# The first two products behind the third and the fifth norm advance together, each split block serving both

## The chip, the cores and the metric

The kernel runs on one core of one Trainium2 chip. The metric is the device time of one execution in microseconds, the median of the runs shown. The engines are named as in the profile: PE is TensorE's matmul, DVE is VectorE, ACT is ScalarE, POOL is GpSimd, SP is SyncE, which here only issues transfers.

## What is computed

The reference is a transformer block with two attention branches and a mixture of experts, followed by a second block. The change touches two places of the second block, and the reference has these lines for them (all in fp32, 1024 positions of 1024 channels):

```python
def second_block(x, p, g_mix_pre, g_mix_post, w_in, ...):
    h = rms_norm(x, g_mix_pre[l])            # the "third norm", n3
    z = h @ w_in[l]                          # 512 pool columns first, then the others
    ...
    x = x + rms_norm(merged @ w_o[l], g_mix_post[l])     # n4
    h = rms_norm(x, g_ffn_pre[l])            # the "fifth norm", n5
    up = h @ w_up[l]
    gate_h = causal_dwconv(up[..., :D_FF], ffn_conv_w[l], ffn_conv_b[l])
    hid = jax.nn.gelu(gate_h) * up[..., D_FF:]
    x = x + rms_norm(hid @ w_down[l], g_ffn_post[l])
```

## The kernel before, in words

Activations lie transposed: channels in 8 row blocks of 128 partitions, 1024 positions along the free axis (`KD` is 8, `D` and `T` are 1024, `HALF` is 512). A fp32 operand is split into a high and a low part. The weights of a product are one tile of 1024 x 128, loaded into `wraw` (SP), split by POOL into `whi` (line 377) and `wlo` (line 379), both with two slots r = 0 and 1. The activations are in `Ah` and `Al`. One product gives 128 output channels for all positions: for each of 8 row blocks j and each half, three matmuls (lines 405 to 407), 48 in all, summed in the PSUM tile `acc[r]`.

Semaphores tie this together. `w_lo` counts split weights. `w_used` counts finished products; POOL splits the weights of product n once `w_used` has reached n - 1, that is, when the product before the last one is finished, whose slot it reuses. `acc_free[r]` counts the times that `acc[r]` was emptied. Every engine runs its own instructions strictly in the order of the program.

A norm's factor is not applied before these products but when their result is read. So a product needs only the split rows of its input, while the mean square and its root can come later.

**Behind the third norm.** PE transposes the experts' rows (`turn(m)`, line 1918, eight transposes each) alternately into `acc[1]` and `XX`. DVE adds the residual (`C`, line 1959), ACT makes `Ah` (line 596), DVE makes `Al` (line 599), the latter one block behind the former. The product `pool` 0 takes the row blocks as they come (it waits on `n3_lo`), with `turn(j + 2)` issued ahead of block j by `ahead`. Product 1 runs as a whole behind it. DVE sums the eight squares in its order behind all eight rows of `Al` (lines 1967 and 1969), against ACT's squares (line 1943) in two buffers. PE then waits for the last sum, forms the mean into `Y` (`add_mean`, line 574), and only then goes on to product 2. Between products 0 and 1 POOL also waits for all eight transposes and clears `bdr` (line 1903), and SP's loads of the products after the fourth are queued behind that. ACT empties `acc[0]` and `acc[1]` (`raw_out`, line 1869) behind its squares.

**Behind the fifth norm.** DVE makes each row of the sum (`C`, lines 2276 and 2277) and one block later its `Al` (line 599). ACT makes `Ah` and the square. PE does block j of product `ffn0` 0 and then adds the mean of row j into `Y` (`after`). Product 1 is issued in the next part of the program. Behind the last mean come ACT's root (lines 582 and 583), DVE's `newton_step` (lines 589 to 591) with the factor `R5`, and then DVE empties `acc[0]` with a multiplication by `R5` (line 2354). Product 2 needs that.

Of the kernel before, what the change touches and what calls it, by code (L numbers as in the profile page):

```python
# [27 lines left out]
KD = D // P  # L28
NB = T // P
HALF = 512  # L30
# [77 lines left out]
N0 = {}  # L108
# [14 lines left out]
def program(nc, A, out):  # L123
# [3 lines left out]
    def S(name):  # L127
        if name not in sems:
            sems[name] = nc.alloc_semaphore(name=name + suffix)
        return sems[name]  # L130
# [18 lines left out]
    whi = alloc("whi", [P, 2, KD, P], F32R, offset=o_whi)  # L149
    wlo = alloc("wlo", [P, 2, KD, P], F32R, offset=o_wlo)  # L150
    Ah = alloc("Ah", [P, KD, T], F32R, offset=o_ah)
    Al = alloc("Al", [P, KD, T], F32R, offset=o_al)
# [29 lines left out]
    def vec(name, j=0, n=1):  # L182
        return VEC[:, VCOL[name] + j:VCOL[name] + j + n]
# [103 lines left out]
    acc = [nc.alloc_psum_tensor(f"acc{i}", [P, T], F32) for i in range(2)]  # L287
    XX = nc.alloc_psum_tensor("XX", [P, T], F32)
    X = [XX[:, i * HALF:(i + 1) * HALF] for i in range(2)]
    Y = nc.alloc_psum_tensor("Y", [P, T], F32)  # L290
# [17 lines left out]
    w_lo, w_used = S("w_lo"), S("w_used")  # L308
    acc_free = [S("acc_free0"), S("acc_free1")]
# [38 lines left out]
    def take(r):  # L348
        taken[r] += 1
        return taken[r] - 1 or None  # L350

    def product_run(pe, n0, n, ih, il, k=KD, k0=0):
        with pe.Fori(0, n // 2) as i:
            for r in range(2):
                product(pe, n0 + 2 * i + r, r, ih, il, k, k0, free=i + taken[r])
        taken[0] += n // 2
        taken[1] += n // 2
# [32 lines left out]
    def product(pe, n, r, ih, il, k=KD, k0=0, m=P, free=None, ready=None, after=None, ahead=None):  # L390

        pe.wait_ge(w_lo, n + 1)
        if free is not None:
            pe.wait_ge(acc_free[r], free)
        for j in range(k):
            if ahead is not None:
                ahead(j)
            if ready is not None:  # L400
                pe.wait_ge(ready[0], ready[1] + j + 1)
            for h in range(2):
                o = acc[r][0:m, h * HALF:(h + 1) * HALF]
                cols = slice(h * HALF, (h + 1) * HALF)
                pe.matmul(o, whi[:, r, j, 0:m], ih[:, k0 + j, cols], start=(j == 0), stop=False)  # L405
                pe.matmul(o, whi[:, r, j, 0:m], il[:, k0 + j, cols], start=False, stop=False)  # L406
                last = pe.matmul(o, wlo[:, r, j, 0:m], ih[:, k0 + j, cols], start=False, stop=(j == k - 1))  # L407
            if after is not None and j < k - 1:
                after(j)
        last.then_inc(w_used, 1)  # L410
        if after is not None:
            after(k - 1)

    def ada_load(sp, dst, q, k, landed_sem):

        sp.dma_start(dst, A["ada_w"][0, k * P:(k + 1) * P, q * D:(q + 1) * D]).then_inc(landed_sem, 16)
# [17 lines left out]
    @block.gpsimd  # L434
    def _(pool):
        ch = chain(pool, "pool")
        for t, v in ((one, 1.0), (eps, EPS), (ident, 0.0), (identb, 0.0), (causb, 0.0), (strict, 1.0), (onesb, 1.0),
                     (meanD, 1.0 / D), (meanH, 0.0)):
            ch(pool.memset(t[:], v))
        ch(pool.memset(meanH[0:HD, 0:HD], 1.0 / HD))  # L440
        ch(pool.memset(meanH[HD:P, HD:P], 1.0 / HD))
        for t in (ident, identb):
            ch(pool.affine_select(out=t[:], in_=t[:], compare_op=ALU.not_equal, fill=1.0, base=0,
                                  pattern=[[-1, P]], channel_multiplier=1))

        ch(pool.affine_select(out=causb[:], in_=causb[:], compare_op=ALU.is_ge, fill=NEG, base=0,
                              pattern=[[-1, P]], channel_multiplier=1))

        ch(pool.affine_select(out=strict[:], in_=strict[:], compare_op=ALU.is_gt, fill=0.0, base=0,
                              pattern=[[1, P]], channel_multiplier=-1))  # L450
        pool.sem_inc(S("setup"), 1)
# [119 lines left out]
    def add_mean(pe, squares, first, last, done):  # L571

        for h in range(2):
            ins = pe.matmul(Y[:, h * HALF:(h + 1) * HALF], meanD[:], squares[:, h * HALF:(h + 1) * HALF],  # L574
                            start=first, stop=last)
        ins.then_inc(S(done), 1)
# [152 lines left out]
    def _(pe):  # L729
# [68 lines left out]
        for n in range(Q0 + 12):  # L798
            product(pe, n, n % 2, Ah, Al, free=take(n % 2), ready=(S("n1_lo"), 0) if n == 0 else None,
                    m=HD + 16 if n == 5 else P, after=lambda k, n=n: between(n, k))  # L800
            if n == 5:
                pe.wait_ge(S("k_norm"), 1)
                mean_of(SQ[:, 0, :], XX, "k_norm")
# [293 lines left out]

    units = [(kind, j, b) for kind in ("fox", "dsa") for j in range(4) for b in range(NB)]
    groups = [[(c, min(4, b + 1 - c)) for c in range(0, b + 1, 4)] for _, _, b in units for _ in range(2)]
    g0 = [sum(len(g) for g in groups[:s]) for s in range(2 * len(units) + 1)]  # L1100
    nmax, psum = (lambda s: att[:, 0, s % 4:s % 4 + 1]), (lambda s: att[:, 1, s % 4:s % 4 + 1])
# [223 lines left out]
    @block.tensor  # L1325
    def _(pe):
        for r in range(2):
            product(pe, N0["proj"] + r, r, Ah, Al, 4, 4 * r, free=take(r), ready=(S("o_lo"), 4 * r))
        with pe.Fori(0, 7) as m:
            for r in range(2):  # L1330
                product(pe, 2 * m + N0["proj"] + 2 + r, r, Ah, Al, 4, 4 * r, free=m + taken[r])
        taken[0] += 7
        taken[1] += 7
        product(pe, N0["wout"], 0, Bh, Bl, free=take(0), ready=(S("merged"), 0))
        product(pe, N0["wout"] + 1, 1, Bh, Bl, free=take(1))
        product_run(pe, N0["wout"] + 2, 6, Bh, Bl)
# [523 lines left out]
    block = stage.enter_context(nc.Block())  # L1860


    turn_banks = (acc[1], XX)
    gain3 = lambda m: vec("g_mix_pre_2", m)

    def raw_out(act, g):
# [45 lines left out]
    @block.tensor  # L1912
    def _(pe):
        def turn(m):
            if m >= 2:
                pe.wait_ge(S("x2_done"), m - 1)
            for b in range(NB):
                last = pe.transpose(turn_banks[m % 2][:, b * P:(b + 1) * P], G12[:, 0, b, m * P:(m + 1) * P], ident[:])
            last.then_inc(S("y_turned"), 1)

        def ahead(j):
            if j + 2 < KD:
                turn(j + 2)

        pe.wait_ge(S("y_sum"), NB)
        turn(0)
        turn(1)
        product(pe, N0["pool"], 0, Ah, Al, free=take(0), ready=(S("n3_lo"), 0), ahead=ahead)
        product(pe, N0["pool"] + 1, 1, Ah, Al, free=take(1))
        pe.wait_ge(S("n3_sum"), KD)  # L1930
        add_mean(pe, TT[:, 2, :], True, True, "n3_mean")

# [374 lines left out]
    @block.tensor  # L2307
    def _(pe):
        def after(j):
            pe.wait_ge(S("n5_sq"), j + 1)  # L2310
            add_mean(pe, TT[:, j % 2, :], j == 0, j == KD - 1, "n5_sum")
        product(pe, N0["ffn0"], 0, Ah, Al, free=take(0), ready=(S("n5_lo"), 0), after=after)

# [2 lines left out]
    for c in range(CH):  # L2318
        n0 = N0[f"ffn{c}"]
# [12 lines left out]
        @block.tensor  # L2332
        def _(pe):
            if c == 0:
                product(pe, n0 + 1, 1, Ah, Al, free=take(1))
                product_run(pe, n0 + 2, 14, Ah, Al)
            else:
                product_run(pe, n0, 16, Ah, Al)
            product(pe, n0 + 16, 0, Bh, Bl, free=take(0), ready=(S("hid_lo"), 8 * c))
            product(pe, n0 + 17, 1, Bh, Bl, free=take(1))  # L2340
            product_run(pe, n0 + 18, 6, Bh, Bl)
# [237 lines left out]
```

## Time and profile before

| | us |
|---|---|
| median of 3 runs | 3582.59 (3578.93 to 3582.71) |
| the profiled execution's own time | 3582.84 |
| its span, from the first to the last instruction | 3581.1 |
| PE busy | 3191.9 (89%) |
| DVE busy | 2170.1 (61%) |
| ACT busy | 1322.4 (37%) |
| POOL busy | 1028.4 (29%) |
| mean granted TensorE clock | 0.949 of full |

The busy shares are means over stages. All times of stretches below count from the start of the span. In a timeline row the columns are: start, duration, engine, line, operation, tile written and tiles read, form, count, and in brackets the idle time of the engine just before, with what ended it. Consecutive matmuls overlap, so what a matmul costs is the distance from its start to the start of the next.

### The profile page before, as it was taken

Reading aid. Unit: us, or ns where it says so; the run is one execution under the profiler, and the core shown is the slowest. Engines: PE = TensorE matmul, PEld = TensorE weight load, DVE = VectorE, ACT = ScalarE, POOL = GpSimd, SP = SyncE. Lnnn points to the kernel's source line nnn. Section 1 sums busy time; section 2 is a strip of 40 time slices with the busy share of each in tenths; the row PEclk is TensorE's granted clock in tenths of the full one; section 3 lists DMA queues with packets and bytes.
Section 4 is the critical chain, followed back from the end, with each engine's and each line's share of the span. In section 5 each row is a group of like instructions: output and inputs, shape, how many; then the busy total and the mean of one; then the engine's idle time right before and its main releaser. Section 6 shows DMA issues by size and latency. Waiting matters only on the chain. (4 is left out here: it accounts for less than half of the span.)

```text
span 3581.1 us, 45184 instructions
## 1 busy us (share of the span) xinstructions
PE 3191.9 (89%) x15078; PEld 2527.7 (71%) x15078; DVE 2170.1 (61%) x2771; ACT 1322.4 (37%) x1726; POOL 1028.4 (29%) x529
## 2 busy tenths in 40 slices
PE   5889988888886399999959999699799999999868
PEld 4658866555674388888848788588588888888647
DVE  6588875786524599999865655633555154154362
ACT  3345423666302388888720364101311000001141
POOL 2223322000231211111124333344244444344332
PEclk9999999999998699999979999899899999999989
DMA  6312221230231599999961122132311111111213
GB/s 223 82 42 89 71 59 47 95 110 10 88 129 56 218 385 381 376 379 386 345 237 47 59 88 66 31 115 79 112 56 50 47 47 50 50 47 47 102 57 117
DMA packets 348590, 454.47 MB, mean 127 GB/s; under 512 B 33662, under 2 KB 230204, under 8 KB 348484
## 3 DMA queue, kind: packets, MB, share of 16 engines
q1 hardware_dynamic: 334420, 422.68, 34.2%
q10 hardware_dynamic: 4192, 13.63, 1.3%
q0 software_dynamic: 9872, 16.81, 1.3%
q8 instruction: 59, 0.97, 0.1%
q14 instruction: 47, 0.39, 0.0%
HBM read 401.58 MB, written 62.98 MB: 130 GB/s over the span
## 5 line engine op out<-in xcount | busy, mean ns | idle before, releaser
L405 PE MATMUL acc<-Ah,whi 128*128 128x512 f32 x2336 | 934.0, 400 | 74.5 <-DVE Al L599 18.5
L377 POOL TENSOR_TENSOR whi<-wraw,one 128x1024 fp32r<-128x1024 f32 (+3 forms) x214 | 394.3, 1842 | 1868.1 <-PE acc L407 1533.8
L406 PE MATMUL acc<-Al,whi 128*128 128x512 f32 x2336 | 918.5, 393 | 0.0
L407 PE MATMUL acc<-Ah,wlo 128*128 128x512 f32 x2336 | 918.3, 393 | 0.0
L405 PEld LDWEIGHTS acc<-Ah,whi 128*128 128x128 f32 x2336 | 443.7, 190 | 193.9 <-issue 69.9
L379 POOL TENSOR_TENSOR wlo<-wraw,whi 128x1024 fp32r<-128x1024 f32 (+3 forms) x214 | 532.9, 2490 | 16.8
L406 PEld LDWEIGHTS acc<-Al,whi 128*128 128x128 f32 x2336 | 444.1, 190 | 97.0 <-issue 5.1
L407 PEld LDWEIGHTS acc<-Ah,wlo 128*128 128x128 f32 x2336 | 443.4, 190 | 95.2
L1785 DVE TENSOR_TENSOR mlo<-mraw,mhi 128x1024 fp32r<-128x1024 f32 x256 | 306.3, 1224 | 36.5 <-ACT mhi L1735 25.1
L1735 ACT ACTIVATE mhi<-mraw 128x1024 fp32r<-128x1024 f32 x256 | 266.7, 1062 | 73.1 <-PE acc L1680 45.9
L405 PE MATMUL acc<-Bh,whi 128*128 128x512 f32 x640 | 251.2, 393 | 9.1 <-POOL wlo L379 9.1
L407 PE MATMUL acc<-Bh,wlo 128*128 128x512 f32 x640 | 250.0, 391 | 0.0
L406 PE MATMUL acc<-Bl,whi 128*128 128x512 f32 x584 | 229.2, 393 | 0.0
L2410 ACT ACTIVATE TT<-TT 128x1024 f32<-128x1024 f32 x24 | 25.4, 1060 | 498.6 <-DVEq L2362 498.6
L1678 PE MATMUL acc<-mhi,XTh 128*128 128x512 f32 x512 | 204.3, 399 | 4.7 <-DVE mlo L1785 3.7
L1679 PE MATMUL acc<-mlo,XTh 128*128 128x512 f32 x512 | 201.2, 393 | 0.0
L1680 PE MATMUL acc<-mhi,XTl 128*128 128x512 f32 x512 | 201.1, 393 | 0.0
L1628 POOL DMA_INDIRECT Xs<-h2rows,IDC x33 | 43.6, 1322 | 427.4 <-DVE IDC L1817 409.7
L1791 DVE TENSOR_TENSOR mlo<-mraw,mhi 128x1024 fp32r<-128x1024 f32 x128 | 148.2, 1220 | 0.4
L405 PEld LDWEIGHTS acc<-Bh,whi 128*128 128x128 f32 x640 | 120.8, 189 | 37.0 <-POOL wlo L379 12.0
L407 PEld LDWEIGHTS acc<-Bh,wlo 128*128 128x128 f32 x640 | 120.8, 189 | 25.5
L1741 ACT ACTIVATE mhi<-mraw 128x1024 fp32r<-128x1024 f32 x128 | 132.5, 1066 | 14.8 <-PE acc L1699 13.0
(446 smaller groups left out, 4785.0 us busy)
## 6 DMA issues: line engine op xcount, KB each, us to landing
mraw<-in_exp_w SPq DMA_DIRECT2D x512, 256.0 KB, 6.5
mraw<-in_exp_w SPq DMA_DIRECT2D x128, 512.0 KB, 12.0
wraw<-in_w_in SPq DMA_DIRECT2D x72, 512.0 KB, 3.7
wraw<-in_w_up SPq DMA_DIRECT2D x48, 512.0 KB, 3.7
TT<-in_ada_w SPq DMA_DIRECT2D x32, 512.0 KB, 3.7
TT<-gates SPq DMA_DIRECT2D x32, 512.0 KB, 4.4
wraw<-in_w_down SPq DMA_DIRECT2D x24, 512.0 KB, 3.5
adaraw<-in_ada_w SPq DMA_DIRECT2D x16, 512.0 KB, 8.5
```

Source lines behind the costliest of these rows:

```text
L377: ch(pool.tensor_tensor(whi[:, r, 0:k, 0:m], wraw[:, r, 0:k, 0:m], one[:, 0:1].unsqueeze(2).broadcast_to([P, k, m]), ALU.mult))
L379: pool.tensor_tensor(wlo[:, r, 0:k, 0:m], wraw[:, r, 0:k, 0:m], whi[:, r, 0:k, 0:m].bitcast(F32), ALU.subtract).then_inc(w_lo, 1)
L405: pe.matmul(o, whi[:, r, j, 0:m], ih[:, k0 + j, cols], start=(j == 0), stop=False)
L406: pe.matmul(o, whi[:, r, j, 0:m], il[:, k0 + j, cols], start=False, stop=False)
L407: last = pe.matmul(o, wlo[:, r, j, 0:m], ih[:, k0 + j, cols], start=False, stop=(j == k - 1))
L1678: pe.matmul(o, XTh[:, k, :], mhi[:, k, cols], start=(k == 0), stop=False)
L1679: pe.matmul(o, XTh[:, k, :], mlo[:, k, cols], start=False, stop=False)
L1680: last = pe.matmul(o, XTl[:, k, :], mhi[:, k, cols], start=False, stop=(k == UPS - 1))
L1735: act.activation(mhi[:, q, :], mraw[:, q, :], ACT.Copy).then_inc(S("up_hi"), 1)
L1741: act.activation(mhi[:, UPS + j, :], mraw[:, UPS + j, :], ACT.Copy).then_inc(S("down_hi"), 1)
L1785: dve.tensor_tensor(mlo[:, q, :], mraw[:, q, :], mhi[:, q, :].bitcast(F32), ALU.subtract)\
L1791: dve.tensor_tensor(mlo[:, q, :], mraw[:, q, :], mhi[:, q, :].bitcast(F32), ALU.subtract)\
```

## The change

A new function `product_pair` runs two products through the row blocks together: at each j it waits once for the row block and issues the 6 matmuls of product n into `acc[0]` and the 6 of product n + 1 into `acc[1]`. It waits for the split weights of both and for both accumulators before anything else. It replaces products 0 and 1 behind the third norm and behind the fifth. The transposes behind the third norm now go to `Y` and `XX`, since `acc[1]` is in use from the start. `take` counts as before.

```diff
+    def product_pair(pe, n, ih, il, ready, ahead=None, after=None):
+        for r in range(2):
+            pe.wait_ge(w_lo, n + r + 1)
+            free = take(r)
+            if free is not None:
+                pe.wait_ge(acc_free[r], free)
+        for j in range(KD):
+            if ahead is not None:
+                ahead(j)
+            pe.wait_ge(ready, j + 1)
+            for r in range(2):
+                for h in range(2):
+                    o = acc[r][:, h * HALF:(h + 1) * HALF]
+                    cols = slice(h * HALF, (h + 1) * HALF)
+                    pe.matmul(o, whi[:, r, j, :], ih[:, j, cols], start=(j == 0), stop=False)
+                    pe.matmul(o, whi[:, r, j, :], il[:, j, cols], start=False, stop=False)
+                    last = pe.matmul(o, wlo[:, r, j, :], ih[:, j, cols], start=False, stop=(j == KD - 1))
+                if j == KD - 1:
+                    last.then_inc(w_used, 1)
+            if after is not None:
+                after(j)
...
-    turn_banks = (acc[1], XX)
+    turn_banks = (Y, XX)
...
-        product(pe, N0["pool"], 0, Ah, Al, free=take(0), ready=(S("n3_lo"), 0), ahead=ahead)
-        product(pe, N0["pool"] + 1, 1, Ah, Al, free=take(1))
+        product_pair(pe, N0["pool"], Ah, Al, S("n3_lo"), ahead=ahead)
         pe.wait_ge(S("n3_sum"), KD)
         add_mean(pe, TT[:, 2, :], True, True, "n3_mean")
...
-        product(pe, N0["ffn0"], 0, Ah, Al, free=take(0), ready=(S("n5_lo"), 0), after=after)
+        product_pair(pe, N0["ffn0"], Ah, Al, S("n5_lo"), after=after)
...
             if c == 0:
-                product(pe, n0 + 1, 1, Ah, Al, free=take(1))
                 product_run(pe, n0 + 2, 14, Ah, Al)
```

## Rows read from the trace of the kernel before

**Rows 1.** The page: busy time of each engine, share of the span, instructions.
```profile
PE 3191.9 (89%) x15078; PEld 2527.7 (71%) x15078; DVE 2170.1 (61%) x2771; ACT 1322.4 (37%) x1726; POOL 1028.4 (29%) x529
```

**Rows 2.** Timeline of DVE behind the third norm: two successive products are emptied.
```profile
1927.97 1.23 DVE L2090 TENSOR_TENSOR TT<-acc,RG 128x1024 f32<-128x1024 f32 x1 [2.50 <-PE acc L407]
...
1938.85 1.23 DVE L2090 TENSOR_TENSOR TT<-acc,RG 128x1024 f32<-128x1024 f32 x1 [2.50 <-PE acc L407]
```

**Rows 3.** Timeline of PE behind the third norm.
```profile
1846.67 1.10 PE L1918 MATMUL acc<-ident,G 128*128 128x128 f32 x8 [0.45 <-POOL wlo L379]
...
1851.92 1.82 PE L1918 MATMUL XX<-ident,G 128*128 128x128 f32 x8
...
1858.04 1.03 PE L1918 MATMUL XX<-ident,G 128*128 128x128 f32 x8
...
1860.68 1.03 PE L1918 MATMUL acc<-ident,G 128*128 128x128 f32 x8
...
1863.38 1.03 PE L1918 MATMUL XX<-ident,G 128*128 128x128 f32 x8
...
1882.32 1.98 PE L574 MATMUL Y<-TT,meanD 128*128 128x512 f32 x4 [1.20 <-DVEq L1970]
...
1895.05 0.39 PE L405 MATMUL acc<-Ah,whi 128*128 128x512 f32 x1
```

**Rows 4.** Chain of work that ended last, there: start, us, what.
```profile
1868.37 0.62 DVE TT L1967
...
1870.49 2.89 DVE TT L1969
1873.51 3.21 DVE TT L1969
...
1880.98 1.24 DVE TT L1969
```

**Rows 5.** Timeline of POOL behind the third norm.
```profile
1848.55 3.25 POOL L379 TENSOR_TENSOR wlo<-wraw,whi 128x1024 fp32r<-128x1024 f32 x1
...
1870.39 1.89 POOL L377 TENSOR_TENSOR whi<-wraw,one 128x1024 fp32r<-128x1024 f32 x1 [4.09 <-PE acc L407]
1872.36 3.27 POOL L379 TENSOR_TENSOR wlo<-wraw,whi 128x1024 fp32r<-128x1024 f32 x1
```

**Rows 6.** Stretches: length, busy time of each engine, PEclk granted, DMA share.
```profile
1850.00:1853.50 3.50, 3.50 (x15) 2.92 (x13) 2.73 (x2) 1.15 (x1) 1.79 (x1) 0.51 0.12 33
...
2572.00:2577.20 5.20, 5.20 (x11) 3.08 (x11) 4.98 (x5) 1.69 (x2) 0.00 (x0) 0.51 0.35 142
...
2555.00:2558.90 3.90, 3.78 (x4) 1.17 (x4) 0.00 (x0) 0.07 (x1) 0.00 (x0) 0.50 0.00 0
```

**Rows 7.** Timeline of PE behind the fifth norm.
```profile
2571.93 0.77 PE L405 MATMUL acc<-Ah,whi 128*128 128x512 f32 x1 [13.13 <-DVE Al L599]
...
2577.20 0.80 PE L405 MATMUL acc<-Ah,whi 128*128 128x512 f32 x1
...
2578.99 1.88 PE L574 MATMUL Y<-TT,meanD 128*128 128x512 f32 x4
2580.30 0.79 PE L405 MATMUL acc<-Ah,whi 128*128 128x512 f32 x1
...
2600.12 1.88 PE L574 MATMUL Y<-TT,meanD 128*128 128x512 f32 x4
...
2612.76 0.39 PE L405 MATMUL acc<-Ah,whi 128*128 128x512 f32 x1
```

**Rows 8.** Timeline of DVE behind the fifth norm: two rows of `Al`, newton, `acc[0]` emptied.
```profile
2582.16 1.28 DVE L599 SCALAR_TENSOR_TENSOR Al<-C,VEC,Ah 128x1024 fp32r<-128x1024 f32 x1
...
2586.05 1.28 DVE L599 SCALAR_TENSOR_TENSOR Al<-C,VEC,Ah 128x1024 fp32r<-128x1024 f32 x1
...
2604.32 1.50 DVE L589 SCALAR_TENSOR_TENSOR TT<-TT 128x1024 f32<-128x1024 f32 x1 [7.65 <-ACTq L584]
...
2608.57 1.23 DVE L2354 TENSOR_TENSOR TT<-acc,TT 128x1024 f32<-128x1024 f32 x1 [0.24 <-DVE TT L591]
```

## The prediction

> **What bounds the kernel now.** I read the page first: PE is busy 3191.9 of 3581.1 us [rows 1]. Steady work there is a row of products. Two are emptied 10.88 us apart, and each time DVE had waited for PE [rows 2]. So a product of 48 matmuls costs 10.88, one matmul 0.2267, six 1.36 and twelve 2.72. While PE sets the pace like this, a delay ahead of it is handed on in full to the end. The question is when product 2 can start in each of the two places, and at which clock.
>
> Behind the third norm I read the timelines of PE and POOL and then the chain. The third transposition, at 1846.67, waited for the first split weights. From then on PE and DVE go nearly in step, 2.64 us for a transposition and a block of six matmuls (1858.04 to 1860.68). The last transposition is at 1863.38, the mean at 1882.32, and product 2 is finished at about 1895.05 [rows 3]. The reader should see who released the mean: DVE's queue, after an idle 1.20. The chain runs through the sum of squares, not through product 1, which filled that time [rows 3, 4].
>
> Behind the fifth norm PE first waits 13.13 for a row of `Al`. A block with its mean then costs 3.10 (2577.20 to 2580.30), of which the mean is 1.31. The last mean starts at 2600.12 and product 2 at 2612.76 [rows 7]. In between lies product 1, and beneath it, hidden, the way from the mean to the emptied `acc[0]`: DVE's first newton step at 2604.32, the emptying at 2608.57 until 2609.80 [rows 8], 9.68 after the mean's start.
>
> **The change, part by part.** No matmul, transposition or transfer is added or removed. Product 1 moves from behind the blocks to between them. That fills PE's waits there, and it makes everything that hung on the end of a block six matmuls later, seven or eight times over. It also uncovers what product 1 covered.
>
> *Third norm, the start.* The pair waits for the second split weights too. POOL finishes them at 1848.55 + 3.25 = 1851.80 [rows 5]. The third transposition is queued behind that wait, so it goes from 1846.67 to about 1851.9, and DVE's next residual row waits for it.
>
> *The clock.* From 1850.0 to 1853.5 the granted clock was 0.51, after a partly idle stretch; behind the fifth norm it was 0.51 until 2577.20, 5.2 us after work began again, and in the mean at 2555.0, which had waited for a sum of DVE's, it was 0.50 [rows 6]. These are the 1.2 GHz level against 2.4. I let each idle stretch of 5 us and more be followed by 5.2 us at half speed, worth 2.6; 3.5 us, worth 1.75, is the lower bound.
>
> *Third norm, the blocks.* At half speed the transposition takes about 1.75 (1.82 lasts the one at 1851.92, 1.03 the ones at full clock [rows 3]), to 1853.65. By 1857.1 eight matmuls are done at 0.43, and the other four take 0.9: the next transposition is at 1858.0 instead of 1851.92. From here a period is 2.64 + 1.36 = 4.00, more than DVE's own, so PE sets it. The last transposition comes four periods later, at 1874.0 instead of 1863.38, or 10.6 late. Blocks 5, 6 and 7 end the pair at 1874.0 + 4.00 + 2 x 2.72 = 1883.4. Product 1 ended at about 1881.1 before (1882.32 less the idle 1.20).
>
> *What is late next: the sum.* DVE adds squares only behind all its rows, so its first sum goes from 1868.37 to about 1879.0. That is the core of my forecast: the pair stretches DVE's rows by what it puts between them, and the sum comes behind them. In the old order the sum had one split of POOL's beside it. Two sums took 2.89 and 3.21 instead of 1.24 [rows 4], while POOL's two instructions ran from 1870.39 to 1875.63 [rows 5], a surcharge of 3.6. Now `w_used` rises for both products within 1.4 us, so POOL does two splits in a row from about 1882.1, in the middle of the sums: between nothing more and a second 3.6. I take the whole, since four POOL instructions and five sums meet. The mean is then 10.6 + 3.6 = 14.2 late, at 1896.5. PE has been idle for 13 us, so mean and product 2 start at half speed: 2.6 more. ACT empties `acc[0]` behind its squares and ahead of the mean as now, and product 2's weights are split by 1888; neither ends last. **Sum: +16.8**, with 11.5 if the surcharge doesn't double and both slow stretches are short (-3.6, -0.85, -0.85), and 19 if the third transposition's stretch also holds up the first rows.
>
> The Trainium skill says of this sharing (SBUF — State Buffer, section "Who interferes with whom") that a DVE instruction with two SBUF inputs and a GpSimd instruction that reads SBUF exclude each other for the whole instruction. By that, the surcharge doubles; by a reading of the rows as one chance collision, it stays at 3.6 and the total falls by 3.6.
>
> *POOL's and SP's queues.* POOL's clearing of `bdr` waits for the last transposition and moves with it, from just behind 1863.38 to about 1875 [rows 3], still 5 us ahead of the next split. SP's loads behind it move by the same 10.6. They serve products from the fifth on, which are far off: nothing.
>
> *Banks.* `Y` in place of `acc[1]` for the transposition: same shapes, and the mean writes `Y` long after its last reader. Nothing. If the bank cost something, it would be within DVE's slack of 4.00 against 2.64 a period.
>
> *Fifth norm, the blocks.* Both weights were split long ago. Block 0 starts at 2571.93 and is now twelve matmuls at half speed, to 2577.2. The mean takes 1.31, to 2578.5. A period is 3.10 + 1.36 = 4.46 against the 3.89 of DVE's three instructions (2582.16 to 2586.05 [rows 8]), so PE sets it again. The last mean starts at 2578.5 + 6 x 4.46 + 3.15 = 2608.4, or 8.3 late [rows 7]. PE is done at 2609.7, three microseconds before the old 2612.76: this is the gain that the pair does make.
>
> *What is late next: the root.* The way from the mean to the emptied `acc[0]` is 9.68 [rows 8], with nothing left to cover it: 2608.4 + 9.7 = 2618.1. POOL's two splits, from 2607.0, now lie beside the newton steps, of which two read two SBUF tiles. The first was held for some 0.3 before (1.50 [rows 8]); held behind one POOL instruction each they cost up to 1.3, as each of the sums did. I take 1.3 of the range 0 to 2.5. Product 2 starts at 2619.4 instead of 2612.76, +6.6, and after an idle 9.7 at half speed, +2.6. **Sum: +9.2**, between 7.0 (no collision, short slow stretch) and 11.
>
> The Trainium skill (TensorE: Matmul & The Clock Gate, section "Loop structure matters more than you think") says that DVE copying a result out of PSUM doesn't break PE's warmth. By that the last 2.6 would be absent and the total 2.6 lower. The rows speak against it here, as PE has nothing else to do: behind the 13.13 that it waited for DVE [rows 7] it got 0.51 [rows 6].
>
> **Total.** 16.8 + 9.2 = 26.0 on the profiled execution's own time of 3582.84 (its span of 3581.1 and 1.7 around it), which is 0.25 above the median: 3608.8, as a median 3608.6. The bounds give 3582.6 + 18.5 = 3601 and 3582.6 + 30 = 3613.
>
> **The rivals.**
> *A, the gain arrives.* What follows isn't uncovered: the sum keeps up with the pair and `acc[0]` is emptied in time. Behind the third norm the pair ends at 1883.4, 2.3 late, or with no slow stretch at 1880.8, 0.3 early; behind the fifth it ends 3.0 early. That is -3.3 to -0.7, 3579 to 3582, not slower. It speaks for it that PE does wait on `Al` in both stretches. Against it: DVE's order puts the sums behind the rows, and 9.68 from the mean to the emptied `acc[0]` has nothing above it. It decides only if both hidden chains end before the pair does: from a last sum at 1883 and a root chain of 1.3 on. To be faster by over 0.2% no mechanism in these rows suffices.
> *B, only the third norm loses.* If the clock doesn't fall in the new waits and the splits don't collide with sums or newton steps, what stays is 10.6 and 5.4 (8.3 + 9.7 less 12.6): +16, 3598.6. For it: one surcharge was all that the sums saw. Against it: rows 6.
> *C, the delay grows.* The half-speed stretch spreads, or DVE's rows are held by POOL's late splits as well: each further slow stretch is 2.6 and each held DVE instruction 1.3 to 2. Five of them give +35, 3617.
>
> **How the numbers follow.** The likeliest, +18.5 to +30, gets 0.77; B, down to +10, 0.11; C 0.05; A 0.04, and a mechanism that I don't see, with a gain over 0.2%, 0.03. The measurement can tell about 0.2% (7 us) from no change. So slower has 0.93, same 0.04, faster 0.03. The range is 3599 to 3615: it holds the likeliest, its bounds, and the upper part of B.
>
> **What would show it.** The third transposition at about 1851.9 and the last at 1874; the first sum at 1879 and its last at about 1895; a wait of PE's for DVE's queue of some 13 us ahead of the mean (1.20 before); PEclk near 0.5 for some 5 us behind it. Behind the fifth norm, the last mean at about 2608.4 plus the delay so far, then a wait of PE's of 8 to 10 us that ends with DVE's line that empties `acc[0]` (in the old numbering 2354). Outside the two places nothing but shifts. The prediction is wrong if the mean waits less than 5 us, or if product 2 behind the fifth norm starts right behind the last mean.

## The result, and the profile after

The changed kernel takes 3607.75 us (median of 4 runs, 3605.04 to 3609.15), against 3580.76 for the kernel before on the same chips (4 runs, 3578.78 to 3582.71). The ratio is 1.0073, 95% interval 1.0061 to 1.0085: slower by 26 us, between 22 and 30 (the two medians differ by 27.0). The profiled execution took 3605.04.

The page of the changed kernel: the span, and the busy time of the engines.

```profile
span 3603.3 us, 45184 instructions
...
PE 3194.9 (89%) x15078; PEld 2532.0 (70%) x15078; DVE 2172.5 (60%) x2771; ACT 1322.2 (37%) x1726; POOL 1027.7 (29%) x529
```

The busy time of PE is nearly the same (3191.9 before [rows 1]), in a span that is 22.2 longer. The loss is waiting, and a few us of half speed.

To compare traces I use two stretches between fixed instructions of DVE. *Stretch 3* runs from the first residual row behind the experts to the first emptying of a product of the next run of products. *Stretch 5* runs from the last emptying of the merged branches to the second emptying of an `ffn0` gate product. Their ends in the kernel before, timeline of DVE:

```profile
1844.62 1.28 DVE L1959 SCALAR_TENSOR_TENSOR C<-acc,MOD,RG 128x1024 f32<-128x1024 f32 x1 [2.20 <-PE acc L1918]
...
1917.01 1.23 DVE L2090 TENSOR_TENSOR TT<-acc,RG 128x1024 f32<-128x1024 f32 x1 [26.22 <-PE acc L407]
...
2462.43 1.22 DVE L2240 TENSOR_TENSOR TT<-TT,acc 128x1024 f32<-128x1024 f32 x1 [8.72 <-PE acc L407]
...
2623.84 1.22 DVE L2354 TENSOR_TENSOR TT<-acc,TT 128x1024 f32<-128x1024 f32 x1 [3.78 <-PE acc L407]
```

And in the changed kernel:

```profile
1843.01 1.28 DVE L1981 SCALAR_TENSOR_TENSOR C<-Y,MOD,RG 128x1024 f32<-128x1024 f32 x1 [2.20 <-PE Y L1941]
...
1929.39 1.23 DVE L2112 TENSOR_TENSOR TT<-acc,RG 128x1024 f32<-128x1024 f32 x1 [26.23 <-PE acc L407]
...
2474.58 1.22 DVE L2262 TENSOR_TENSOR TT<-TT,acc 128x1024 f32<-128x1024 f32 x1 [8.73 <-PE acc L407]
...
2645.37 1.22 DVE L2375 TENSOR_TENSOR TT<-acc,TT 128x1024 f32<-128x1024 f32 x1 [4.30 <-PE acc L407]
```

Stretch 3 went from 72.39 to 86.38, +13.99; stretch 5 from 161.41 to 170.79, +9.38. The trace of the changed kernel runs 1.61 early at its start (1843.01 against 1844.62), and one adds that when comparing its times with rows of before.

**Behind the third norm**, timeline of PE in the changed kernel, to be read beside [rows 3]:

```profile
1850.34 1.94 PE L1941 MATMUL Y<-ident,G 128*128 128x128 f32 x8 [5.74 <-POOL wlo L379]
...
1856.34 1.03 PE L1941 MATMUL XX<-ident,G 128*128 128x128 f32 x8
...
1859.98 1.04 PE L1941 MATMUL Y<-ident,G 128*128 128x128 f32 x8
...
1870.86 1.03 PE L1941 MATMUL XX<-ident,G 128*128 128x128 f32 x8
...
1893.13 3.55 PE L597 MATMUL Y<-TT,meanD 128*128 128x512 f32 x4 [12.65 <-DVEq L1992]
```

The third transposition waited 5.74 for POOL's second split. The periods are 3.64 (1856.34 to 1859.98), of which the twelve matmuls take 2.85, from 1857.13 on; before, six took 1.50 (1859.18 to 1860.68). So a matmul in the pair costs no more than one outside it, which leaves rival P of the experiments below (the blocks themselves are dearer) nothing to stand on here. The mean waited 12.65 for DVE's last sum, where it had waited 1.20 before, and its four records take 3.55 instead of 1.98, at half speed. The sums of DVE and the splits of POOL in the same stretch, timelines, to be read beside [rows 4, 5]:

```profile
1876.60 16.43 DVE L1991 TENSOR_TENSOR TT<-TT 128x1024 f32<-128x1024 f32 x7
...
1879.27 1.89 POOL L377 TENSOR_TENSOR whi<-wraw,one 128x1024 fp32r<-128x1024 f32 x1 [5.50 <-PE acc L431]
1881.24 3.21 POOL L379 TENSOR_TENSOR wlo<-wraw,whi 128x1024 fp32r<-128x1024 f32 x1
1884.41 2.87 POOL L377 TENSOR_TENSOR whi<-wraw,one 128x1024 fp32r<-128x1024 f32 x1
1887.36 3.21 POOL L379 TENSOR_TENSOR wlo<-wraw,whi 128x1024 fp32r<-128x1024 f32 x1
```

Two splits now stand back to back beside the sums.

**Behind the fifth norm**, timeline of PE, beside [rows 7]:

```profile
2584.07 0.76 PE L429 MATMUL acc<-Ah,whi 128*128 128x512 f32 x1 [13.13 <-DVE Al L622]
...
2590.60 0.80 PE L429 MATMUL acc<-Ah,whi 128*128 128x512 f32 x1
...
2595.07 0.79 PE L429 MATMUL acc<-Ah,whi 128*128 128x512 f32 x1
...
2620.68 1.88 PE L597 MATMUL Y<-TT,meanD 128*128 128x512 f32 x4
...
2631.64 0.80 PE L405 MATMUL acc<-Ah,whi 128*128 128x512 f32 x1 [9.08 <-DVEq L2376]
```

A period is 4.47 (3.10 before), the last mean comes 36.61 behind the first block (28.19 before), and product 2 then waits 9.08 for the emptied `acc[0]`. The timeline of DVE shows the way there, beside [rows 8]:

```profile
2624.87 1.91 DVE L612 SCALAR_TENSOR_TENSOR TT<-TT 128x1024 f32<-128x1024 f32 x1 [12.32 <-ACTq L607]
...
2630.30 1.22 DVE L2375 TENSOR_TENSOR TT<-acc,TT 128x1024 f32<-128x1024 f32 x1 [0.24 <-DVE TT L614]
```

The stretches from the two restarts on show the clock, beside [rows 6]. The columns are length, the busy times of PE, PEld, DVE, ACT and POOL, then PEclk, the busy share of DMA and its GB/s:

```profile
1893.10:1896.50 3.40, 3.37 (x5) 1.50 (x5) 0.00 (x0) 0.00 (x0) 0.00 (x0) 0.53 0.20 60
2631.60:2637.00 5.40, 5.36 (x13) 4.26 (x14) 4.60 (x4) 1.06 (x1) 0.00 (x0) 0.50 0.13 40
```

PEclk is 0.53 and 0.50, the 1.2 GHz level: for about 3.4 us and 5.4 us both restarts run at half speed.

### The profile page after: what moved, and what is told of

Read it like the earlier page. It is cut to its first block and busy times, and to the rows that moved or that the text cites. A ratio compares the mean times of both kernels' runs of the same rounds, so it can differ in the third digit from the quotient of the medians.

```text
span 3603.3 us, 45184 instructions
## 1 busy us (share of the span) xinstructions
PE 3194.9 (89%) x15078; PEld 2532.0 (70%) x15078; DVE 2172.5 (60%) x2771; ACT 1322.2 (37%) x1726; POOL 1027.7 (29%) x529
## 5 line engine op out<-in xcount | busy, mean ns | idle before, releaser
L405 PE MATMUL acc<-Ah,whi 128*128 128x512 f32 x2272 | 907.4, 399 | 65.0 <-DVEq L2188 14.8
L406 PE MATMUL acc<-Al,whi 128*128 128x512 f32 x2272 | 895.1, 394 | 0.0
L407 PE MATMUL acc<-Ah,wlo 128*128 128x512 f32 x2272 | 894.4, 394 | 0.0
L405 PEld LDWEIGHTS acc<-Ah,whi 128*128 128x128 f32 x2272 | 432.6, 190 | 176.2 <-issue 54.2
L379 POOL TENSOR_TENSOR wlo<-wraw,whi 128x1024 fp32r<-128x1024 f32 (+3 forms) x214 | 533.3, 2492 | 16.8
L406 PEld LDWEIGHTS acc<-Al,whi 128*128 128x128 f32 x2272 | 432.5, 190 | 93.7 <-issue 4.3
L407 PEld LDWEIGHTS acc<-Ah,wlo 128*128 128x128 f32 x2272 | 432.0, 190 | 92.1
```

The source lines that it names most:

```text
L379: pool.tensor_tensor(wlo[:, r, 0:k, 0:m], wraw[:, r, 0:k, 0:m], whi[:, r, 0:k, 0:m].bitcast(F32), ALU.subtract).then_inc(w_lo, 1)
```

## The experiments

The stretches of all traces, in us, with the time of the median run and the ratio to the kernel before on the same chip:

| kernel | stretch 3 | stretch 5 | median | ratio (95%) |
|---|---|---|---|---|
| before | 72.39 | 161.41 | 3580.76 | |
| before, second trace | 72.26 | 161.41 | 3579.11 (one run) | |
| the change | 86.38 | 170.79 | 3607.75 | 1.0073 (1.0061 to 1.0085) |
| the change, second trace | 86.39 | 170.79 | 3608.03 (one run) | |
| third norm alone | 86.85 | 161.45 | 3596.43 | 1.0043 (1.0026 to 1.0060) |
| fifth norm alone | 72.26 | 170.75 | 3590.89 | 1.0031 (1.0019 to 1.0042) |
| mean behind product 2 | 84.03 | 170.47 | 3604.45 | 1.0069 (1.0053 to 1.0086) |
| fourth split later | 82.94 | 170.84 | 3602.50 | 1.0061 (1.0044 to 1.0078) |
| PE kept busy | 86.78 | 169.08 | 3604.37 | 1.0070 (1.0055 to 1.0085) |
| pair's waits later | 83.23 | 170.48 | 3600.44 | 1.0057 (1.0042 to 1.0073) |
| third norm alone, two repairs | 81.30 | 161.41 | 3591.53 | 1.0031 (1.0019 to 1.0042) |
| one block put between | 74.59 | 160.08 | 3585.66 | 1.0015 (1.0006 to 1.0024) |
| mean behind product 2, emptying earlier | 77.18 | 171.12 | 3598.06 | 1.0051 (1.0036 to 1.0066) |
| one block put between, emptying earlier | 71.07 | 160.05 | 3580.13 | 0.9998 (0.9989 to 1.0007) |

A time differs from another of the same kernel by up to 9 us (the kernel before ran from 3575.3 to 3584.7 on one chip); in two traces of one kernel the two stretches repeat within 0.13. Between kernels with the same code in a place they differ more: 86.38 and 86.85 for stretch 3, 170.47 to 171.12 for stretch 5. So a stretch tells 1 us apart, which a median can't.

**Each place alone.** In the first kernel the fifth norm has its two products as before, in the second the third norm.

```diff
-        product_pair(pe, N0["ffn0"], Ah, Al, S("n5_lo"), after=after)
+        product(pe, N0["ffn0"], 0, Ah, Al, free=take(0), ready=(S("n5_lo"), 0), after=after)
...
+                product(pe, n0 + 1, 1, Ah, Al, free=take(1))
```

> The pair behind the third norm alone; the fifth norm's part is as in the kernel before. Theory U (each pair uncovers a chain that product 1 had covered: the sum of squares here, the root there) says the two places are independent: this one costs 14.0 us, as the trace of the change shows between the first transposition and the first emptied product behind it, so about 3595. Rival P (the pair's own blocks are dearer, through the weight slots or the bank Y, wherever they stand) says the same here, since the blocks are the same. Rival D (one place's delay is partly made up, or made worse, by the other) says that this run and the next do not add up to the change.

> The pair behind the fifth norm alone. Theory U: +9.4 us (last mean 8.4 late, acc[0] emptied another 1.2 late, 2.7 for the half-speed stretch behind the idle 9.1, less the 3.1 by which the pair ends early is no gain), so about 3590. Rival D: under 6 or over 13, and the sum with the run before is not that of the change (about 26).

Stretch 3 alone +14.46, stretch 5 alone +9.34, and each leaves the other where it was (161.45 and 72.26). The medians, 1.0043 and 1.0031, add up to 1.0074 against 1.0073. The places are independent within this accuracy, so rival D falls.

**The mean behind product 2.** PE does product 2 before it waits for the sum.

```diff
-        pe.wait_ge(S("n3_sum"), KD)
-        add_mean(pe, TT[:, 2, :], True, True, "n3_mean")
...
-        product_run(pe, N0["pool"] + 2, 10, Ah, Al)
+        product(pe, N0["pool"] + 2, 0, Ah, Al, free=take(0))
+        pe.wait_ge(S("n3_sum"), KD)
+        add_mean(pe, TT[:, 2, :], True, True, "n3_mean")
+        product(pe, N0["pool"] + 3, 1, Ah, Al, free=take(1))
+        product_run(pe, N0["pool"] + 4, 8, Ah, Al)
```

> The change, with PE's wait for the last sum and the mean of the third norm moved from ahead of product 2 to behind product 2. Theory U: PE no longer waits 12.65 us for the sum. Product 2 then waits for POOL's split, which ends about 5.2 us after product 0's last matmul, so some 4 us behind the pair's end. Product 2 starts 8 to 9 us earlier than in the change and without the half-speed stretch of 1.6: 9 to 10 us faster than the change, about 3598. Rival P: the loss is in the pair's blocks, at most 3 us come back, about 3605.

Only 2.35 came back in stretch 3 (86.38 to 84.03), not 9 to 10. My expectation failed, and rival P's figure was the one met. The timelines of PE, ACT and POOL in this kernel say why:

```profile
1889.18 0.76 PE L405 MATMUL acc<-Ah,whi 128*128 128x512 f32 x1 [10.14 <-POOL wlo L379]
...
1887.98 1.01 ACT L1892 ACTIVATE UP<-acc 128x1024 f32<-128x1024 f32 x1
...
1879.80 3.21 POOL L379 TENSOR_TENSOR wlo<-wraw,whi 128x1024 fp32r<-128x1024 f32 x1
...
1885.92 3.21 POOL L379 TENSOR_TENSOR wlo<-wraw,whi 128x1024 fp32r<-128x1024 f32 x1
```

Product 2 waited 10.14, put down to POOL's split. But the split for product 2 was finished at 1883.01 (1879.80 + 3.21). The one for product 3 ended at 1889.13, 0.05 ahead of the start; product 2 doesn't wait for it, as the next run shows. What ended at 1888.99, 0.19 ahead of the start, is ACT's emptying of `acc[0]`. It stands behind ACT's eight squares, and these wait for DVE's sums. So a second way from the sums to product 2 lay close beneath the first: in the change ACT is done with `acc[0]` 2.7 ahead of the mean.

Of the 2.35, some 0.6 lie ahead of the sums, where nothing was edited: these start 32.98 behind the first residual row (1875.20 less 1842.22) against 33.59 in the change (1876.60 less 1843.01).

**That way tested.** The same kernel, with ACT's emptying of `acc[0]` behind its fifth square.

```diff
             act.activation(TT[:, m % 2, :], C[:, m, :], ACT.Square).then_inc(S("n3_sq"), 1)
-        for g in range(2):
-            raw_out(act, g)
+            if m == 4:
+                raw_out(act, 0)
+        raw_out(act, 1)
```

> The change with the mean of the third norm behind product 2, and ACT's emptying of acc[0] placed behind its fifth square instead of behind its eighth. The run with the mean behind product 2 gave 2.4 us in that stretch where theory U had expected 9 to 10, and in its trace product 2 started 0.2 us behind ACT's emptying of acc[0], which stands behind squares that wait for the sums. Theory Q (that queue of ACT's is the second thing that product 1 covered): product 2 now starts when POOL's split is done, 6 us earlier, so the stretch from the first residual row to the first emptied product of the next run falls from 84.0 to 77 or 78 us, and the time to about 3597. Rival P (the pair's blocks, or the clock behind the wait, are the rest): the stretch stays above 82.

Stretch 3 fell by another 6.85 to 77.18, and the median to 3598.06. Timelines of PE, ACT and POOL:

```profile
1884.14 0.50 PE L405 MATMUL acc<-Ah,whi 128*128 128x512 f32 x1 [4.02 <-POOL wlo L379]
...
1879.93 1.00 ACT L1892 ACTIVATE UP<-acc 128x1024 f32<-128x1024 f32 x1
...
1880.88 3.21 POOL L379 TENSOR_TENSOR wlo<-wraw,whi 128x1024 fp32r<-128x1024 f32 x1
```

Now POOL's split for product 2 really ends last, at 1884.09, and product 2 starts while the split for product 3 still runs. The two edits gave back 9.2 of the 14.0 us of stretch 3, 0.6 of them by the scatter between builds. So the larger part of the loss is the ways that lead through the sums, and rival P is out as its cause. What is left, 4.8, holds the late third transposition (tested below), PE's wait of 4.02 for the split, and the lower clock behind this wait (0.63 for 4.6 us).

**The fourth split later.** POOL's split for product 3 waits for the last sum.

```diff
+            if j == 3:
+                pool.wait_ge(S("n3_sum"), KD)
             split(pool, N0["pool"] + j, j % 2, landed[N0["pool"] + j])
```

> The change, with POOL's fourth split (for product 3) made to wait until the third norm's sum is done, so that only one split lies beside the sums. Theory U with the surcharge per split: the seven sums take 13.1 us as before instead of 16.4, the mean comes 3.3 us earlier, and product 3's split still ends under product 2: 3.3 us faster than the change, about 3604. Rival S (the surcharge comes from something else than POOL, such as ACT's squares): the sums stay at 16.4 and the time at 3607.

Timeline of DVE:

```profile
1878.12 13.03 DVE L1993 TENSOR_TENSOR TT<-TT 128x1024 f32<-128x1024 f32 x7
```

The seven sums take 13.03 instead of 16.43, and stretch 3 is 3.44 shorter. So a second split beside the sums costs 3.4, and the surcharge comes from POOL, as expected against rival S. The Trainium skill (SBUF — State Buffer, section "Who interferes with whom") says that a DVE instruction with two SBUF inputs contends with a GpSimd instruction that reads SBUF, and that the ports they share are an exclusive lock. The traces agree: the two held sums of before took 1.65 and 1.97 longer than the free one of 1.24 [rows 4], each about as long as one POOL instruction of 1.89 [rows 5].

**PE kept busy.** Matmuls that nobody reads fill PE's two waits; they are work added to the computation, in the unused bank `XX`.

```diff
+    def keep_busy(pe, n):
+        for i in range(n):
+            pe.matmul(X[i % 2], meanD[:], C[:, 0, 0:HALF], start=True, stop=True)
...
         product_pair(pe, N0["pool"], Ah, Al, S("n3_lo"), ahead=ahead)
+        keep_busy(pe, 18)
...
         product_pair(pe, N0["ffn0"], Ah, Al, S("n5_lo"), after=after)
+        keep_busy(pe, 12)
```

> The change, with matmuls that nobody reads issued into the free bank XX in PE's two waits: 18 of fp32 128x512 between the pair and the third norm's mean, 12 behind the fifth norm's last mean, at 0.65 us each some 11.8 and 7.8 us, less than the idle 12.65 and 9.1. Theory U with the clock as a term: the waits end at the same time, but what follows runs at full clock: 1.6 us back behind the third norm and 2.7 behind the fifth, 4.3 us faster than the change, about 3603. Rival K (the granted clock falls all the same, or the wait itself is all of the loss): no difference, 3607.

Timeline of PE in both places and the stretches behind them (columns as above):

```profile
1879.24 15.61 PE L416 MATMUL XX<-C,meanD 128*128 128x512 f32 x36
1894.69 1.88 PE L601 MATMUL Y<-TT,meanD 128*128 128x512 f32 x4
...
2624.29 10.46 PE L416 MATMUL XX<-C,meanD 128*128 128x512 f32 x24
...
2634.19 0.79 PE L405 MATMUL acc<-Ah,whi 128*128 128x512 f32 x1
...
1894.70:1898.00 3.30, 3.30 (x12) 2.07 (x11) 0.00 (x0) 1.36 (x2) 0.00 (x0) 1.00 0.00 0
...
2634.00:2639.00 5.00, 5.00 (x22) 3.81 (x21) 4.37 (x4) 1.06 (x1) 0.00 (x0) 1.00 0.04 12
```

The added matmuls took 0.87 us each (15.61 for 18), not 0.65, and overran the wait. Behind the third norm the mean started 52.21 behind the first residual row (1894.69 less 1842.48), against 50.12 in the change: 2.09 later. Stretch 3 is only 0.40 longer, so 1.69 came back through the clock, which was 1.00 behind the added matmuls. Behind the fifth, product 2 started 11.61 behind the last mean (2634.19 less 2622.58), against 10.96 in the change, and stretch 5 is nevertheless 1.71 shorter. From the start of product 2 to the end of the stretch it took 11.53 instead of 13.73. So the clock's share is shown, 1.7 and 2.2. The kernel before needs 11.08 for the last part; the 0.45 between is a longer first matmul behind the added ones. As a repair it can't be told from nothing at this length: the ratio, 1.0070, is inside the change's interval.

**The pair's waits later.** Each product's weights and accumulator are waited for ahead of its own first block.

```diff
-        for r in range(2):
-            pe.wait_ge(w_lo, n + r + 1)
-            free = take(r)
-            if free is not None:
-                pe.wait_ge(acc_free[r], free)
         for j in range(KD):
             ...
             for r in range(2):
+                if j == 0:
+                    pe.wait_ge(w_lo, n + r + 1)
+                    free = take(r)
+                    if free is not None:
+                        pe.wait_ge(acc_free[r], free)
```

> The change, with the pair's waits moved: the split weights of product n are waited for ahead of its own first block and those of product n + 1 ahead of its first block, both behind the transposition. Theory U with the start as a term: the third transposition starts at about 1846.7 instead of 1852 (in the frame of the kernel before), the fourth at about 1854.5 instead of 1858: 3 to 4 us faster than the change, about 3604. Rival W (the start doesn't matter, as DVE's rows or the clock take it back): within 1 us of the change.

Stretch 3 is 3.15 shorter, as expected; the median, 3600.44, fell by more than the 3 to 4 us forecast. The third transposition stands 1.40 behind the first residual row (1841.97, first of its records, less 1840.57) instead of 7.33 (1850.34 less 1843.01). The start was a term of its own. It was worth more than 3.15 up to the mean, which stands 45.54 behind the first residual row (1886.11 less 1840.57) instead of 50.12, or 4.58 earlier. Behind it 1.4 were lost again: from the mean to the end of the stretch it takes 37.69 instead of 36.26, and the clock from 1886 to 1892 was 0.50.

**Both repairs on the third norm alone.**

> The pair behind the third norm alone, with the mean behind product 2 and the waits moved as in the two runs that do one of these each; the fifth norm as in the kernel before. Theory U: the losses are the chains, so with both repaired the pair costs what is left, the wait of product 2 for its split weights: 0 to 2 us over the kernel before. Rival P: the pair's blocks are dearer in themselves, over 5 us above the kernel before.

Stretch 3 was 81.30, +8.91, not 0 to 2. The expectation failed, and by its words this was rival P's result. But the kernel leaves ACT's queue as it was: it has the same wait in front of product 2, 10.13 us, and product 2 starts at 1888.46, 0.19 behind ACT's emptying (1887.27 + 1.00). So it is no evidence for rival P. The pair with all three repairs was not run, and whether it would reach the kernel before is not shown.

**One block put between.** Products 0 and 1 stand one behind the other; only the first block of product 1 is taken forward, behind block 4 of product 0, in both places. The mean of the third norm is behind product 2. `fill` is (4,) in both places, and what is left out waits once for the weights and the accumulator of product 1.

```diff
+            block(0, j)
+            if after is not None:
+                after(j)
+            if j in fill:
...
+                block(1, done)
+                done += 1
+        for j in range(done, KD):
+            block(1, j)
```

> Products 0 and 1 one behind the other as in the kernel before, but with a single block of product 1 put into PE's waits behind block 4, in both places; behind the third norm the mean behind product 2 and the transpositions to Y and XX. Theory U: product 1's other seven blocks still cover the root chain (9.52 us against 9.68) and POOL's split. Gains: about 1.3 for the block behind the fifth norm, 1.3 behind the third, 1.2 for PE's wait for the sum: 3 to 4 us faster than the kernel before, about 3577, at the edge of what can be measured. Rival P: any block put between costs more than it saves: at or above the kernel before.

Behind the fifth norm it did what was expected: 160.08, 1.33 shorter than before. The way from the last mean to the emptied `acc[0]` is there as it was (9.68), seven blocks of product 1 lie above it, and PE doesn't wait for it: so it was the missing cover that cost 9.08 of waiting in the change. Behind the third norm the kernel lost 2.2, and the median, 3585.66, is 5 us above the kernel before instead of the 3 to 4 below that I had expected. Another 2.9 of this are in the tail, from the last emptying of an `ffn` gate product to the end (307.39 against 304.46), which the edit doesn't touch. The timeline of PE, and the stretch behind (columns as above):

```profile
1881.91 0.47 PE L405 MATMUL acc<-Ah,whi 128*128 128x512 f32 x1 [1.95 <-ACTq L1929]
...
1881.90:1886.00 4.10, 4.09 (x11) 3.25 (x12) 1.97 (x1) 1.03 (x1) 4.02 (x2) 0.58 0.00 0
```

PE waited 1.95 for ACT to empty `acc[0]`, the same queue, and this short idle stretch was followed by 0.58 of the clock. In the 12.5 us before the wait PE had been busy for 12.47, at 1.00.

**The same, emptying earlier** (`raw_out(act, 0)` behind the fourth square).

> The kernel with one block of product 1 put between, with ACT's emptying of acc[0] placed behind its fourth square. Without this the stretch behind the third norm was 2.2 us longer than in the kernel before, with a wait of 1.95 for ACT and half speed behind it, and the one behind the fifth norm 1.3 shorter. Theory Q: wait and half speed go, the stretch falls from 74.6 to about 71 (72.4 in the kernel before), and the time is about 3 us below the kernel before, 3577 to 3578. Rival P: the stretch stays at 74 or more.

```profile
1879.00:1892.00 13.00, 13.00 (x58) 10.62 (x57) 5.19 (x4) 3.04 (x3) 6.24 (x3) 1.00 0.21 61
```

PE is busy without a gap at full clock. Stretch 3 is 71.07 and stretch 5 160.05, 1.3 and 1.4 below the kernel before. But the median is 0.9998 of it (0.9989 to 1.0007): no difference that can be measured. Neither the expected 3577 to 3578 nor a gain came. In its trace 1.5 us are lost from the first gate to the last `rg` product (321.71 against 320.25 and 319.82 in the two traces of before) and 2.1 in the tail (306.60 against 304.46 and 304.42). I know no cause for these. Nor do the runs part the three things that this kernel changes behind the third norm (the block, the mean behind product 2, the earlier emptying): its 1.3 there belong to the three together.

**Second traces of the kernel before and of the change.**

> The kernel before once more, for a second trace. It shows how much of a difference between two traces outside the two places is scatter: the start of the first transposition behind the experts (1842.5 and, in the others, 1838 to 1843), the stretch of the rg products (119.8 or 121.0) and the tail (302 to 307). If these vary in it too, they belong to no change.

> The change once more, for a second trace. Theory U: behind the third norm 86.4 us and behind the fifth 170.8, as in the first trace, within 0.5; whatever else differs is scatter.

The start of the second block is scatter: the first residual row of the kernel before is at 1844.62 in one trace and 1841.56 in the other, of the change at 1843.01 and 1846.02. The tail is not: 304.46 and 304.42 in the kernel before, 305.13 and 305.15 in the change. Of the `rg` stretch, of which I had expected 121.0 now and then, both kernels have 119.8 or 119.9 in both traces. Such differences of up to 3 us go with the build, not with the execution.

## Why the prediction was right

Forecast 3608.6, measured 3607.75; forecast +26.0, measured +26 (22 to 30). The two stretches give 13.99 + 9.38 = 23.4, the tail 0.7, together 24.1. From the first residual row to the end the two traces of before take 1736.5 and 1735.8, the two of the change 1760.3 and 1760.3: 23.8 to 24.5. So the mechanism was right and my total about 2 us too large. Nearly all of the excess is in the third norm, 16.8 against 13.99. That the medians came closer than this (+27.0) is luck of the scatter. Step by step:

- *The start.* Third transposition forecast at 1851.9; 1850.34 + 1.61 = 1851.95. That it costs was shown by moving the waits: 4.58 up to the mean, 3.15 in the end.
- *The blocks behind the third norm: mis-sized.* I took 4.00 for a period and it was 3.64. The 2.64 of the old period was the pace of DVE, which had no idle time between its rows there and 0.9 a period in the change. PE alone needs 3.64 less 1.36, or 2.28. The last transposition came at 1870.86 + 1.61 = 1872.47, 9.1 late instead of 10.6.
- *The sum.* Late by 9.1 at its start, plus 3.3 for the second split (3.6 forecast), and the mean 12.4 late (14.2 forecast). The surcharge is shown by the run with the fourth split later.
- *"ACT empties `acc[0]` behind its squares and ahead of the mean as now": it doesn't end last, but with little room.* ACT was done with `acc[0]` at 1890.41, 2.7 ahead of the mean. I had priced the wait at the mean and not what lies beneath it, which made two of my later expectations wrong.
- *The clock.* Forecast 2.6 behind each wait. Behind the third norm half speed lasted 3.4 us and the loss was 1.6 (13.99 less 12.42 for the mean), a little under my lower bound of 1.75; behind the fifth 5.4 us and 2.7 (13.73 less 11.08). Keeping PE busy gave back 1.7 and 2.2. With the blocks (1.5) and the sum (0.3), this 1.0 makes up the 2.8 by which the third norm was put too high.
- *The fifth norm.* Last mean 8.4 late (8.3 forecast), `acc[0]` emptied 1.2 late on top (1.3), product 2 6.7 late (6.6), half speed 2.7 (2.6): 9.4 against 9.2. The first and third newton steps took 1.91 and 1.99 beside POOL's late splits, 0.4 and 0.8 more than before. I had put a held step at 1.3, "as each of the sums did", but the sums had been held for 1.65 and 1.97 [rows 4]; that the total fits is partly luck. The uncovered root chain is shown by PE's wait of 9.08 and by its absence where seven blocks lie above the same chain. The pair with the chain out of the way would need a third accumulator and wasn't tried.
- *The copy out of PSUM.* The Trainium skill (TensorE: Matmul & The Clock Gate, section "Loop structure matters more than you think") has DVE's copy leave PE warm in a loop whose next matmuls follow immediately. Here they can't follow, since they need the emptied `acc[0]`: PE's 9.08 us of waiting for it were followed by 0.50 of the clock.
- *Rival A* is out: both chains end long behind the pair. *Rival B* is out: splits collide and the clock falls. *Rival C*: nothing of it.

## What to carry to other kernels

Work that stands behind a dependent chain covers what follows that chain. Before moving it into the waits ahead, list everything that it covered and how long each way is: here DVE's sums, ACT's queue behind them, POOL's next split, the root and the emptying, and PE's clock. Fill a wait only by as much as the wait is long. Eight blocks between lengthened the stretches by 14 and 9 us. One block shortened stretch 5 by 1.3; behind the third norm it first cost 2.2, and 1.3 were gained only once ACT's emptying stood earlier too. The whole kernel didn't become measurably faster by it. A period read from a trace is the pace of the slowest engine; it can't be taken as the cost of the one that will be slowest after the change. When a wait is put down to one engine, compare the ends of everything that it waits for: the 10.14 put down to POOL was a wait for ACT.

## What the runs showed of the hardware

- An idle stretch of only 1.95 us in front of a product, behind 12.5 us of nearly full work at 1.00, was followed by a granted clock of 0.58 for 4.1 us.
- A fp32 matmul 128x512 costs 0.87 us in a row of its kind (15.61 for 18), although two of them between other matmuls take 1.31 to the next start. I had taken the latter for the price; the rest of it shows in the longer first matmul behind them (0.80 instead of 0.39).
- Two traces of one build agree within 0.5 us over stretches of 70 to 550 us, except in the stretch up to the end of the experts, where they differ by 3 us. Another build of nearly the same program can differ by 0.6 to 3 us in places that the edit doesn't touch.
